# Small products of three attention stages regrouped between dense rows, and four PSUM banks in turn for gated linear attention

## What is computed

```
# differential attention, head h, query block qb (128 queries), c = 0, 1
s  = q_c k_c^T / 8 + alibi;  pr_c = softmax(s);  o = (pr_0 - lam pr_1) v;  o = rmsnorm(o)

# GLA, chunk c of 64 tokens, head h; b = cumsum of log a inside the chunk
q_dec = q * dk^-0.5 * exp(b);  k_in = k * exp(-b);  k_out = k * exp(b_last - b)
attn  = causal(q_dec k_in^T)
state = exp(b_last) * state + k_out^T v          # 8 chunks in turn
o     = attn v + q_dec state;  o = o * rsqrt(mean(o*o))

# dilated attention, group g, head h, four blocks of 128 queries
p = exp(q k^T * hd^-0.5 + bias - max);  o = p v / sum(p);  lse = max + log(sum)
```

## Time and profile before

| | us |
|---|---|
| median of 3 runs | 2126.29 |
| lowest, highest | 2119.96, 2127.86 |
| the profiled execution | 2122.81 |
| its span in the trace | 2120.9 |
| PE busy in it | 2039.4 |
| DVE, ACT, POOL busy | 994.1, 783.3, 293.1 |

### The profile page before, as it was taken

The page is one execution under the profiler, slowest core; times in us unless marked ns, Lnnn a source line. Parts: engine busy times, 40 slices in busy tenths (PEclk is TensorE's granted clock), DMA queues, the critical chain, the costliest instruction groups (busy, mean ns, idle before and its releaser), DMA issues.

```text
span 2120.9 us, 27569 instructions
## 1 busy us (share of the span) xinstructions
PE 2039.4 (96%) x11518; PEld 1625.5 (77%) x11518; DVE 994.1 (47%) x1534; ACT 783.3 (37%) x1233; POOL 293.1 (14%) x292
## 2 busy tenths in 40 slices
PE   7999999999999999999899999998999999999996
PEld 5767677777888778888676788886788888888884
DVE  5665555444643233346845444446643442333354
ACT  5573222113444323235523233335332343322344
POOL 2001221210221001012200000001310220100124
PEclk9999999899999999999999999999999999999998
DMA  4121111112623332223321122221222233222221
GB/s 174 60 70 60 46 52 41 46 42 76 209 87 109 112 102 90 99 100 119 120 67 56 57 70 80 82 88 60 82 97 100 100 120 109 100 90 99 100 80 50
DMA packets 59843, 185.46 MB, mean 87 GB/s; under 512 B 6551, under 2 KB 11799, under 8 KB 59592
## 3 DMA queue, kind: packets, MB, share of 16 engines
q1 hardware_dynamic: 59720, 183.71, 25.5%
HBM read 173.46 MB, written 10.22 MB: 87 GB/s over the span
## 4 chain that ended last, share of the span: by engine, by line
PE 85%; DVE 5%; ACT 4%; issue 3%; POOL 1%; DMA 1%; SPq 0%; DVEq 0%; POOLq 0%; ACTq 0%
PE P L545 24%; PE P L547 23%; PE P L546 23%; DVE AREN L1649 1%; PE P L820 1%; PE P L856 1%; PE P L910 1%; PE P L849 1%; DVE WLO L1656 1%; POOL AREN L2318 1%; PE P L908 1%; PE P L805 1%; ACT WHI L1104 1%; POOL AREN L2321 1%; DVE AREN L1652 1%
## 5 line engine op out<-in xcount | busy, mean ns | idle before, releaser
L545 PE MATMUL P<-HH,WHI 128*128 128x512 f32 x1528 | 628.7, 411 | 22.1 <-DVE WLO L1656 11.8
L547 PE MATMUL P<-HH,WLO 128*128 128x512 f32 x1528 | 602.4, 394 | 0.0
L546 PE MATMUL P<-HL,WHI 128*128 128x512 f32 x1528 | 601.5, 394 | 0.0
L1656 DVE TENSOR_TENSOR WLO<-RAW,WHI 128x1024 fp32r<-128x1024 f32 x303 | 382.3, 1262 | 180.4 <-ACT WHI L1104 178.6
L1104 ACT ACTIVATE WHI<-RAW 128x1024 fp32r<-128x1024 f32 x303 | 318.8, 1053 | 377.3 <-PE P L547 374.3
L545 PEld LDWEIGHTS P<-HH,WHI 128*128 128x128 f32 x1528 | 290.2, 190 | 102.8 <-issue 20.2
L545 PE MATMUL P<-ARR,WHI 128*128 128x512 f32 (+1 forms) x904 | 352.1, 390 | 6.5 <-DVE WLO L1656 2.9
L547 PE MATMUL P<-ARR,WLO 128*128 128x512 f32 (+1 forms) x904 | 350.7, 388 | 0.0
L546 PE MATMUL P<-ARR,WHI 128*128 128x512 f32 (+1 forms) x904 | 350.7, 388 | 0.0
L547 PEld LDWEIGHTS P<-HH,WLO 128*128 128x128 f32 x1528 | 290.3, 190 | 63.6
L546 PEld LDWEIGHTS P<-HL,WHI 128*128 128x128 f32 x1528 | 290.9, 190 | 54.7 <-issue 1.2
(11 more groups left out here) (297 smaller groups left out, 1559.3 us busy)
## 6 DMA issues: line engine op xcount, KB each, us to landing
RAW<-in_w_in_dram SPq DMA_DIRECT2D x118, 512.0 KB, 3.3
RAW<-in_w_ff_dram SPq DMA_DIRECT2D x64, 512.0 KB, 3.3
RAW<-in_w_ml_dram SPq DMA_DIRECT2D x64, 512.0 KB, 3.2
RAW<-in_w_out_dram SPq DMA_DIRECT2D x16, 512.0 KB, 3.4
RAW<-in_w_pg_dram SPq DMA_DIRECT2D x16, 512.0 KB, 3.2
AREN<-in_xT_dram SPq DMA_DIRECT2D x16, 256.0 KB, 6.4
s_gates<-AREN SPq DMA_DIRECT2D x16, 256.0 KB, 2.0
RAW<-in_w_ab_dram SPq DMA_DIRECT2D x8, 512.0 KB, 3.5
```

What stands on the lines that cost most here:

```text
L545: e.matmul(out, hi, H[0][:, s], start=first, stop=False)
L546: e.matmul(out, hi, H[1][:, s], start=False, stop=False)
L547: return e.matmul(out, lo, H[0][:, s], start=False, stop=last)
L1656: e.tensor_tensor(WLO[n % NSPL][:, :], RAW[n % NRAW][:, :], WHI[n % NSPL][:, :].bitcast(F32), ALU.subtract).then_inc(*D.dve.sig("wlo", n))
```

## The change

In `weave_order` the steps stand ahead of fewer rows. In GLA the seven `kv` stand at two places instead of four, `kt` is put off from row r + 9 to r + 13 and shares it with `at`, `o` goes from r + 24 to r + 26, and `ss` from r + 27 to r + 32, which is the row of the next head's `a` (for the last head, the row of the first dilated head). In dilated attention the first steps of a head stand together, and `pv` stands at the row of the next head's `vt`. In differential attention three `qk` stand at r and three at r + 3, and all four `pt` at r + 18. GLA's steps take four banks in turn (2, 3, 6, 7) instead of two, on PE, ACT and DVE. On ACT the exponential of b_last - b comes ahead of that of -b. No instruction is added or taken away.

```diff
     for r in (39, 62, 85, 108):
         late = r > 39
-        put("a", r, r, *((r,) if late else ()), r + 2, r + 2, r + 4, r + 4, *((r + 4,) if late else ()), r + 6, r + 6,
-            r + 11, *((r + 12,) if r < 108 else ()), r + 18, r + 18, r + 20, r + 20)
+        put("a", r, r, r, *((r,) if late else ()), r + 3, r + 3, r + 3, *((r + 3,) if late else ()), r + 6, r + 6,
+            r + 11, *((r + 12,) if r < 108 else ()), r + 18, r + 18, r + 18, r + 18)
...
     for h in range(4):
         r = A_GL + 32 * (h + 1) + 1
-        put("g", r, r + 4, r + 4, r + 9, r + 11, r + 13, r + 13, r + 16, r + 16, r + 19, r + 19, r + 22, r + 24, r + 24, r + 27)
+        put("g", r, r + 4, r + 4, r + 13, r + 13, *[r + 17] * 4, *[r + 20] * 3, r + 26, r + 26, r + 32)
     for n in range(12):
+
         r = A_DL + 33 if n == 0 else A_DL + 24 * (n + 1) + 2
-        put("l", *((r, r + 2, r + 2, r + 7, r + 12, r + 12, r + 16) if n < 4 else (r, r, r + 5, r + 11, r + 16)))
+        a, b, c = (6, 12, 17) if n == 0 else (7, 13, 18) if n == 11 else (8, 16, 24)
+        put("l", *((r, r, r, r + a, r + b, r + b, r + c) if n < 4 else (r, r, r + a, r + b, r + c)))
...
             def gla():
-                ring = (2, 3)
+                ring = (2, 3, 6, 7)
...
-                    b = ring[i[0] % 2]
+                    b = ring[i[0] % 4]
...
-                    return bank((2, 3)[(i[0] - 1) % 2])
+                    return bank((2, 3, 6, 7)[(i[0] - 1) % 4])
...
                     w.wait_ge(G.dve.at("d", h))
+                    e.activation(gD, gD, ACT.Exp, scale=1.0 / 16).then_inc(*G.act.sig("d", h))
                     e.activation(gS, gS, ACT.Exp, scale=-1.0 / 16).then_inc(*G.act.sig("n", h))
-                    e.activation(gD, gD, ACT.Exp, scale=1.0 / 16).then_inc(*G.act.sig("d", h))
```

## The result

The changed kernel took 2110.3 us (median of 5 executions, 2103.5 to 2110.7), the kernel before beside it 2125.9 (5, 2120.0 to 2127.9). The ratio is 0.993, with a 95% interval of 0.991 to 0.9949: 15 us faster, where 2109 was forecast. The profiled execution took 2110.7 with a span of 2108.8, so by the traces 12.1 us went.

What follows compares the result with a forecast made beforehand. PE, busy for 96% of the span, was taken as the bound. 13.0 - 0.5 + 3.3 + 0.8 - 0.4 + 0.4 = 16.6 us off 2126.3 gave 2109.7, stated as 2109, range 2098 to 2118.

Steps and rivals of the forecast that it cites:

- kt and the clock: In GLA, four PE waits at kt go (9.7 us), and two clock falls after them (3.3 us): 13.0 us saved.
- The 0.5 for `at`: In GLA, at may wait for DVE's k: 0.15 us in three heads, 0.5 us lost in all, bounds 0 to 3.
- kv: In GLA, seven kv at two places instead of four save 0.8 us a head, 3.3 us in all.
- the two readings of the earlier trace: For GLA's kv: 0.4 us charged once a place (3.3 us saved), or each further pass as slow as the first (0).
- ss: In GLA, ss five rows later finds its input ready and costs 0.85 us instead of 1.05: 0.8 us saved in four.
- Dilated attention: Its 16 fewer places give 0; at the last place the second l waits for bank 5, 0.4 us lost.
- Differential attention: Its 8 fewer places give 0; head 4's pv wait goes (0.6 us), pt may wait 0.2: 0.4 us saved.
- The partial wait: Rival, chance 0.17: GLA's k_out or k comes 1.5 us later than worked out, costing 5 to 7 us: 2116.
- Every place giving something: Rival, chance 0.10: the 32 places not yet counted give 0.2 to 0.4 us each, 6 to 13 more: about 2099.
- The clock falling in the longer places: Rival, chance 0.06: dilated attention's longer runs of small products bring clock falls of 1.6 us each; slower, 2137.

Runs made afterwards that it cites:

- e2: Kernel before with only differential attention's steps regrouped; 2124.6 us, ratio 1.001.
- e3: Kernel before with only dilated attention's steps regrouped; 2118.2 us, ratio 0.9983.
- e5: Changed kernel, but GLA's small products take banks 2 and 3 in turn again instead of four banks; 2113.9 us, ratio 0.9962.
- e9: Changed kernel with ss of the last GLA head three rows earlier and the RWKV products four rows later; 2103.3 us, ratio 0.9916.
- e11: e9 with differential attention in the order of the kernel before; 2104.3 us, ratio 0.992.
- e1: Kernel before with only GLA's part of the change: its order, four banks and the exchanged exponentials; 2105.4 us, ratio 0.9922.

## Why the prediction was right, and where it was not

**kt and the clock (forecast 13.0 less 0.5).** Right. `kt` and `at` cost 3.8 us a head and 4.5 in the two heads where the clock fell; they cost 1.26 now. That is 11.4 us, and about 2 more went with the slower dense rows behind the two falls. k_out was done 11.2 us behind S, the start of `ss` (11.45 forecast), PE came at 11.7, as forecast. The 0.5 for `at` didn't come: 1.26 is the sum of `kt` and `at` within 0.02. The three kernels with the wait (before, e2, e3) have two, one and two falls in the GLA stretch; the ten without it have none from there up to 1450. So it is the wait that took the clock here.

**kv (3.3).** Right: 3.33 us a head became 2.53, 3.2 in all. Of the two readings of the earlier trace rows, the one that charged 0.4 once a place was right. The Trainium skill, page "TensorE: Matmul & The Clock Gate", Part 3, says that weight loads overlap matmuls in flight only where the row group differs. The traces speak against it here: the second pair of `kv` takes 0.43 us, the same as the first, with the row groups of the first. What the forecast only argued, that the banks would be free, e5 shows to be needed: without the two new ones the places cost 4.7 a head.

**ss (0.8).** 0.2 in each of the three heads where `ss` joins `a` (1.96 us against 1.06 and 1.10), so 0.6. In the fourth it was the step that failed: I asked where `ss` comes from and who waits for its product, but not which banks are held until the norm is done, and who takes them next. Price 1.14 us. The forecast looked for such a collision at the other end of dilated attention, where it found one.

**Dilated attention (0, less 0.4 at the end).** Right. Its places cost the sum of their steps within 0.02 to 0.04: `pv`, `vt` and two `qk` 3.53 us against 1.57, 0.45 and 1.53 apart. The last place lost 0.3, of which 0.16 is idle (forecast 0.4).

**Differential attention (0.4).** The places were right (scores cost the same grouped), and so was `pv` in head 4: no wait of 0.57. But the gain stopped at the next wait on ACT, which the trace of before shows with 1.80 us of idle, at the first product behind attention. It was a gain of PE time ahead of a point that PE didn't set. With that wait out of the way, e9 against e11, the regrouping gives 0.6 to 0.7. The same wait, at 2.8, then came with a fall of the clock. I had asked "what is late next" for GLA and not here.

**The sum.** GLA and dilated attention by rows: 13.4 + 3.2 + 0.6 - 1.1 - 0.3, and 0.3 from small differences, so 16.1, against 16.2 forecast for them. That a forgotten loss (1.1) and an overcautious charge (0.5) nearly cancel is luck. The other 0.4, differential attention's, did not come. The time of 2110.3 instead of 2109 is nearer than the method deserves: the clock's falls outside the two stages moved the profiled time by several microseconds between kernels that are the same there (RWKV's rows and the next stage's together took 412.7 us before, 405.3 in e3 and 415.5 in e1), and the executions of one kernel lie 6 to 13 us apart.

**The rivals.** The partial wait didn't come; its margin was 0.5 us at `kt` and nothing at `at`. Every place giving something is refuted by the sums in dilated attention. The clock falling in the longer places is refuted: 3.5 us of small products without a dense row between, and no 0.50 up to 1450 us. But the clock did take part back, at a place that I hadn't looked at, behind a wait and not inside a long place.

**Open.** What decides a fall behind a wait of 2.5 or so isn't settled. The wait of 2.6 us at the last attention head's `ss` had no fall behind it in before and e3, and one in e1, which differs from before only from row 1113 on; of the six kernels with the longer RWKV wait five have it. The falls at 185.4 and 240.0 are in e1 too (186.0 and 240.7). So the RWKV falls of the changed kernel at 161.5, 185.4 and 240.0 can't be put down to the change, while the one at 137.6 goes with the longer wait. And not every fall has a wait ahead of it: at 240.0 PE had been busy since a wait of 1.2 us that ended at 231.1.

## What to carry to other kernels

Before steps are grouped, price one place from two rows: if its passes explain all of it, grouping gives nothing (here full-array products), and if a part is left over (0.4 us for products on 64 of the rows), that part is what a place saves, provided that the group has a bank for each product until the first is emptied. After a gain, walk down the same engine to the next wait and ask who releases it: time won ahead of a wait on another engine is idle time there. And when a step that ends a chain is moved, list the banks that stay full until the chain ends, and who takes them next.

## What the runs showed of the hardware

- Two-pass fp32 products on the whole array take 0.112 us a pass of 128 columns whether they stand alone or in a group of 44 passes; `kv`, a product on 64 rows, costs about 0.4 us more, once for each place (0.83 us for one pair, 1.27 for two). That this is the change of shape is an inference from the spacing of the starts.
- The weight loads of a second pair of 64-row products cost nothing visible behind the first pair on the same rows (0.43 us more for the pair, loads included). With a bank missing, a wait of 0.47 us cost the place 1.3: the idle column shows less than half of what a broken pair costs.
- The clock fell to 0.50 after a wait of 2.3 us in GLA in five of twelve cases (before, e2, e3), at the RWKV product with 2.8 us in six of six, with 1.8 in none of three. A fall of 3.4 us costs about 1.6 us: with three of them RWKV's rows took 140.8 us in e1, with none 136.0 in before, for the same instructions and waits.
